# Half of a depthwise convolution moved from GpSimd to TensorE inside a triangular inversion

## The reference, cut to what matters

```python
def _conv_group(z, conv_w, conv_b, ln_g, ln_b):
    u = z[..., :CONV_CH] * jax.nn.sigmoid(z[..., CONV_CH:])
    u = lax.conv_general_dilated(u, conv_w[:, None, :].astype(u.dtype), window_strides=(1,),
                                 padding=[(CONV_K - 1, 0)], dimension_numbers=('NWC', 'WIO', 'NWC'),
                                 feature_group_count=CONV_CH) + conv_b
    return jax.nn.silu(_layernorm(u, ln_g, ln_b))
...
        z = _rms(h, norm1_g[l]) @ w_in[l]
...
        h = h + jnp.concatenate([ya, yr, yc], axis=-1) @ w_out[l]
        h = h + _peer(_rms(h, norm2_g[l]), peer_wq[l], peer_keys[l], peer_u[l], peer_v[l])
```

## Time and profile before

| what | us |
|---|---|
| median of 3 runs | 2104.95 |
| lowest, highest run | 2094.97, 2105.49 |
| profiled execution, its own time | 2105.58 |
| its span | 2103.4 |
| TensorE busy | 1977.3 (94%) |
| VectorE busy | 1459.2 (69%) |
| GpSimd busy | 1279.7 (61%) |
| ScalarE busy | 962.2 (46%) |

### The profile page before, as it was taken

The page is one execution under the profiler, slowest core; times in us unless marked ns, Lnnn a source line. Parts: engine busy times, 40 slices in busy tenths (PEclk is TensorE's granted clock), DMA queues, the critical chain, the costliest instruction groups (busy, mean ns, idle before and its releaser), DMA issues.

```text
span 2103.4 us, 43605 instructions
## 1 busy us (share of the span) xinstructions
PE 1977.3 (94%) x16516; PEld 1889.8 (90%) x16516; DVE 1459.2 (69%) x2757; ACT 962.2 (46%) x1646; POOL 1279.7 (61%) x667
## 2 busy tenths in 40 slices
PE   9957999999999999999999577999999999999999
PEld 8845899999999999999988467999999999999998
DVE  3864419994777788788748535199627777887886
ACT  5422545554333455545554124455543333555553
POOL 5896469998666633233058964799976666332430
PEclk9966899999999999999999678999999999999999
DMA  5300356665444599899743002566555446998995
GB/s 188 102 1 1 92 170 189 181 180 170 151 143 147 180 339 313 288 313 315 249 135 106 1 1 82 179 192 186 183 169 151 145 146 202 349 322 303 323 328 158
DMA packets 106380, 387.80 MB, mean 184 GB/s; under 512 B 11808, under 2 KB 12064, under 8 KB 106016
## 3 DMA queue, kind: packets, MB, share of 16 engines
q1 hardware_dynamic: 87840, 319.25, 47.3%
q0 software_dynamic: 18432, 67.12, 9.2%
HBM read 385.27 MB, written 1.05 MB: 184 GB/s over the span
## 4 chain that ended last, share of the span: by engine, by line
PE 60%; POOL 24%; issue 13%; DVE 2%; ACT 1%; POOLq 0%; ACTq 0%
PE ps L895 60%; POOL w_lo L552 14%; POOL arena L568 6%; POOL arena L577 4%; DVE x L1386 0%; DVE x_lo L1379 0%; POOL arena L564 0%; ACT w_hi L635 0%; DVE onehots_j L1374 0%; DVE h L1816 0%; DVE sel L1702 0%; ACT L759 0%; ACT L610 0%; DVE h L1815 0%; DVE sel L1705 0%
## 5 line engine op out<-in xcount | busy, mean ns | idle before, releaser
L895 PE MATMUL ps<-x_hi,w_hi 128*128 128x240 f32 (+5 forms) x4768 | 1429.3, 324 | 20.4 <-POOL w_lo L552 10.7
L895 PE MATMUL ps<-x_hi,w_lo 128*128 128x240 f32 (+3 forms) x4768 | 1307.3, 274 | 0.0
L552 POOL TENSOR_TENSOR w_lo<-w,w_hi 128x1024 fp32r<-128x1024 f32 x346 | 871.3, 2536 | 390.6 <-ACT w_hi L635 390.0
L895 PEld LDWEIGHTS ps<-x_hi,w_hi 128*128 128x128 f32 x4768 | 904.2, 190 | 73.5 <-POOL w_lo L552 12.6
L895 PEld LDWEIGHTS ps<-x_hi,w_lo 128*128 128x128 f32 x4768 | 909.3, 191 | 0.0
L635 ACT CAST w_hi<-w 128x1024 fp32r<-128x1024 f32 x596 | 623.5, 1046 | 344.3 <-DMA w<-v_c 204.6
L895 PE MATMUL ps<-x_lo,w_hi 128*128 128x240 f32 (+3 forms) x2720 | 757.1, 278 | 0.0
L895 PEld LDWEIGHTS ps<-x_lo,w_hi 128*128 128x128 f32 x2720 | 519.0, 191 | 0.2
L1773 DVE TENSOR_TENSOR w_lo<-w,w_hi 128x1024 fp32r<-128x1024 f32 x250 | 305.6, 1222 | 114.5 <-ACT w_hi L635 113.7
L895 PE MATMUL ps<-arena 64*64 64x64 f32 (+9 forms) x2496 | 176.7, 277 | 60.9 <-ACT arena L783 19.7
L895 PEld LDWEIGHTS ps<-arena 64*64 64x64 f32 (+6 forms) x2496 | 152.0, 172 | 83.7 <-ACT arena L783 20.4
(11 more groups left out here) (187 smaller groups left out, 1691.7 us busy)
## 6 DMA issues: line engine op xcount, KB each, us to landing
w<-u_c SPq DMA_DIRECT2D x256, 512.0 KB, 3.6
w<-v_c SPq DMA_DIRECT2D x256, 512.0 KB, 5.5
w<-w_c SPq DMA_DIRECT2D x84, 512.0 KB, 3.6
arena<-keys_c SPq DMA_DIRECT2D x2, 1024.0 KB, 5.6
arena<-mix_c SPq DMA_DIRECT2D x2, 792.0 KB, 8.2
h<-h SPq DMA_DIRECT2D x2, 544.0 KB, 4.4
out<-x SPq DMA_DIRECT2D x4, 256.0 KB, 2.1
arena<-lora_c SPq DMA_DIRECT2D x2, 256.0 KB, 9.1
```

Source lines behind the costliest of these rows:

```text
L552: g.tensor_tensor(low_of(l, n, wlo_t), low_of(l, n, wraw_t), high_of(l, n).bitcast(F32), ALU.subtract).then_inc(s_lo, 1)
L895: return nc.tensor.matmul(out_, lhsT, rhs, start=start, stop=stop, skip_group_check=True)
```

## The change

The second block of channels (j = 1) is convolved on TensorE. GpSimd builds 31 matrices of 128 by 128, each the identity times one tap's column of weights; they lie in free parts of the arena, of `sel` and of the two one-hot buffers. TensorE multiplies each with the input shifted by the tap and adds all 31 up in bank 6 in fp32. These products stand at fixed places in the inversion (`FILL`): four ahead of level 0, one ahead of each X, two ahead of each pair of updates, until 31 are issued. The update of the second head pair goes to bank 4 in place of 6. ScalarE adds the bias while it copies the result to `cacc`, and TensorE waits for that copy before it uses bank 6 again. The first block stays on GpSimd; its multiplications now have a second operation in each tap (add 0.0), and its additions cover one block. GpSimd splits the low parts of 18 tiles ahead of the convolution, and those of the next three behind it.

```diff
@@ -36,6 +36,10 @@
 LEVELS = (1, 2, 4, 8, 16, 32)
 CONV_K = 31
 CPAD = CONV_K - 1
+TAPS = (12, 6, 7, 6)
+CONV_BANK = 6
+UP_BANKS = (5, 4)
+FILL = (4, 1, 2)
 AH = 8
 
 PH = 8
@@ -283,6 +287,10 @@
 
         ident, ones, iota, fold = res("ident"), res("ones"), res("iota"), res("fold")
 
+        def tap(k):
+            t, i = tap_at[k]
+            return t[:, i * P:(i + 1) * P]
+
         def vcol(l, name, i=0, parts=slice(0, P)):
             a = VEC[name][0] + i
             return vecs[parts, l, a:a + 1]
@@ -327,6 +335,8 @@
         A.at = over_prep
         gram = A.take(NCH * 2 * 4 * CHUNK).rearrange("p (c j m t) -> p c j m t", c=NCH, j=2, m=4)
         cm = A.take(2 * TP).rearrange("p (j c t) -> p j c t", j=2, c=NCH)
+        tap_t = (A.take(TAPS[0] * P), sel_t[:, NR:NR + TAPS[1] * P], ohA_t[:, 0:TAPS[2] * P], ohB_t[:, 0:TAPS[3] * P])
+        tap_at = [(t, i) for t, n in zip(tap_t, TAPS) for i in range(n)]
 
         A.at = over + 6 * T
         vkb = A.take(NCH * 5 * 2 * HD).rearrange("p (c m j n) -> p c m j n", c=NCH, m=5, j=2)
@@ -557,26 +570,20 @@
                 times(pool, n0, n1, lambda n, it: low(l, n, it))
 
             for l in range(DEPTH):
-                lows(l, 0 if l == 0 else AHEAD, NZ + AHEAD)
+                lows(l, 0 if l == 0 else AHEAD, NZ)
 
                 pool.wait_ge(s_ea, l * (NZ + NQ) + ZQ)
                 link(g.memset(cu[:, :, 0:CPAD], 0.0))
                 link(g.tensor_tensor(cu[:, :, CPAD:CPAD + T], z[:, ZCU:ZCU + 2, 1:T + 1], cacc[:, :, :], ALU.mult))
                 for k in range(CONV_K):
-                    for j in range(2):
-                        dst = cacc if k == 0 else ctmp
-                        ins = g.tensor_scalar(dst[:, j, :], cu[:, j, k:k + T], vcol(l, "conv_w", j * CONV_K + k),
-                                              vcol(l, "conv_b", j) if k == 0 else None, ALU.mult,
-                                              *((ALU.add,) if k == 0 else ()))
-                        if j == 0:
-                            ins.then_inc(s_gl, 1)
-                            link.n += 1
-                        else:
-                            link(ins)
+                    g.tensor_scalar(tap(k), ident, vcol(l, "conv_w", CONV_K + k), 0.0, ALU.mult, ALU.add).then_inc(s_tap, 1)
+                for k in range(CONV_K):
+                    link(g.tensor_scalar((ctmp if k else cacc)[:, 0, :], cu[:, 0, k:k + T], vcol(l, "conv_w", k),
+                                         0.0 if k else vcol(l, "conv_b", 0), ALU.mult, ALU.add))
                     if k:
-                        ins = g.tensor_tensor(cacc[:, :, :], cacc[:, :, :], ctmp[:, :, :], ALU.add)
+                        ins = g.tensor_tensor(cacc[:, 0, :], cacc[:, 0, :], ctmp[:, 0, :], ALU.add)
                         link(ins) if k < CONV_K - 1 else ins.then_inc(s_conv, 1)
-                lows(l, NZ + AHEAD, NP)
+                lows(l, NZ, NP)
                 pool.wait_ge(s_ix, l + 1)
                 pool.wait_ge(s_use, l * NW + NV0)
                 pool.wait_ge(s_gm, G0[l + 1])
@@ -783,6 +790,9 @@
                         nc.scalar.copy(xm[:, j], src).then_inc(s_xc, 1)
                     for _ in range(5):
                         after(steps)
+                act.wait_ge(s_cps, l + 1)
+                nc.scalar.activation(cacc[:, 1, :], ps[:, CONV_BANK, 0:T], ACT.Identity,
+                                     bias=vcol(l, "conv_b", 1)).then_inc(s_cpc, 1)
                 for k, (c0, cn, bank) in enumerate(WU):
                     if bank != WU_DVE:
                         act.wait_ge(s_wu, len(WU) * l + k + 1)
@@ -995,6 +1005,15 @@
                     last.then_inc(s_to, 1)
                     yield
 
+            def convolution(l):
+
+                for k in range(CONV_K):
+                    pe.wait_ge(s_tap, CONV_K * l + k + 1)
+                    last = mm(ps[:, CONV_BANK, 0:T], tap(k), cu[:, 1, k:k + T], k == 0, k == CONV_K - 1)
+                    if k == CONV_K - 1:
+                        last.then_inc(s_cps, 1)
+                    yield
+
             def x_split(l, k):
 
                 return lambda c: pe.wait_ge(s_xl, (3 * l + k) * DC + c + 1)
@@ -1104,18 +1123,25 @@
                                  lambda r, j: vtok[r, c, j, :], c % 4 == 0)
                 last.then_inc(s_x0, 1)
                 nlev = len(LEVELS) - 1
+                taps = convolution(l)
+                for _ in range(FILL[0]):
+                    after(taps)
                 for b in range(nlev):
                     for j in range(2):
 
+                        for _ in range(FILL[1]):
+                            after(taps)
                         pe.wait_ge(s_ti, 2 * nlev * l + 2 * b + j + 1)
                         product(3 + j, cm, ti, j).then_inc(s_x, 1)
                     after(steps)
                     for j in range(2):
 
+                        for _ in range(FILL[2]):
+                            after(taps)
                         pe.wait_ge(s_xc, 2 * nlev * l + 2 * b + j + 1)
                         pe.wait_ge(s_tt, 2 * (nlev + 1) * l + 2 * b + j + 1)
                         if b < nlev - 1:
-                            product(5 + j, tt_, xm, j).then_inc(s_up, 1)
+                            product(UP_BANKS[j], tt_, xm, j).then_inc(s_up, 1)
                         after(steps)
                         if b == 0:
                             pe.wait_ge(s_x0c, 2 * (l + 1))
@@ -1136,6 +1162,9 @@
                                 last = mm(ps[r, bank, at:at + P].rearrange("p (m n) -> p m n", m=2), tt_[r, j, c, :],
                                           vkb[r, c, 3:5, j, :], True, True)
                     last.then_inc(s_wu, 1)
+                for _ in taps:
+                    pass
+                pe.wait_ge(s_cpc, l + 1)
                 for c in range(NCH - 1):
                     quads(part(6, c), lambda r, j: vtok[r, c, j, :], lambda r, j: gram[r, c, j, 1, :], c == 0)
                 after(steps)
@@ -1558,7 +1587,7 @@
                             (2 * (2 * nlev - 1) * l + 4 * b + j - 1)
                         if not last:
                             dve.wait_ge(s_up, up + 1)
-                            v.tensor_tensor(ti[:, j], ti[:, j], update(5 + j), ALU.subtract).then_inc(s_ti, 1)
+                            v.tensor_tensor(ti[:, j], ti[:, j], update(UP_BANKS[j]), ALU.subtract).then_inc(s_ti, 1)
                         after(steps)
                         dve.wait_ge(s_up, up + 2)
                         v.tensor_tensor(tt_[:, j], tt_[:, j], update(7 - 7 * j), ALU.subtract).then_inc(s_tt, 1)
```

More of the change, by code:

```diff
@@ L464, in trunk @@
         s_conv = sem("conv_done")
+        s_tap = sem("conv_tap_matrices_ready")
+        s_cps = sem("conv_second_block_in_psum")
+        s_cpc = sem("conv_second_block_copied")
         s_gl = sem("pool_link")
```

## The result

The median of 13 runs is 2112.09 us (2106.14 to 2116.77), against 2103.53 us of 13 runs of the kernel before on the same chips; the ratio is 1.0048 (95% interval 1.0035 to 1.0061). The change made the kernel slower by 0.48%, about 10 us, where 5 us less were forecast. The profiled execution took 2109.26 us, 2107.1 of them span.

What follows compares the result with a forecast made beforehand. VectorE, then TensorE, bounds the inversion; GpSimd's convolution arrives last only once, by 2.00 us. VectorE's relief −11, taps +14.2, clock −8.3 sum to −5.1 us: 2105.58 to 2100.5 us, range 2086 to 2112.

Steps and rivals of the forecast that it cites:

- GpSimd's own times: GpSimd's convolution beside the inversion: rounds about 1.45 us, tap matrices 0.3 to 0.6 us each, end near 135 us.
- The wait for the convolution: TensorE's 2.00 us wait before layer 0's norm sums goes, but not from the path: 0, other end 2 us.
- ScalarE's copy: Copy of the finished block, about 0.4 us, in ScalarE's idle time ahead of the solved pairs: 0, or 0.4 us.
- the three moved subtractions: Three weight subtractions on GpSimd, now behind the convolution, done by 162 us at worst, ahead of the output projection: no cost.
- the net of taps and clock: Inversion on TensorE: taps on the path add 14.2 us, the risen clock gives back 8.3 us.
- VectorE's relief: Inversion: VectorE's instructions meet fewer and shorter GpSimd additions; 2 × (3 + 1.8 + 0.7) = 11 us gained.
- The first stretch: Level 0 and most of level 1, VectorE the path: 3 us gained per layer, ends 0 and 6.2.
- The other parts: VectorE's late delays at L1459 and L1599, 1.8 us per layer, and L1523's form at the start, 0.7.
- The collision model: First 24.5 us: an arriving VectorE instruction loses 0.26 us on average to GpSimd's additions before, 0.16 after.
- the taps lengthen the path: Levels 1 to 3: 16 taps at 0.91 us, no clock regained; +11.8, 2117 us; chance 0.14.

Runs made afterwards that it cites:

- one-tap kernel with late subtractions: The change with one tap product on TensorE in place of 31, and GpSimd's three subtractions held back until ScalarE's copy; 0.9973 of the kernel before, 2096.31 us.
- one tap: The change with one tap product on TensorE in place of 31, subtractions right behind the convolution; 1.0007 of the kernel before, 2102.76 us.
- free places: The change with its 31 taps moved to other places in the inversion; alone 0.9987 of the kernel before, 2096.87 us; with subtractions late 0.9955, 2092.91 us.
- products with zeros: Taps moved, subtractions late, plus 12 zero-matrix products per layer ahead of the updates of levels 1 to 3; 0.9991 of the kernel before, 2097.94 us.
- base: The change with its taps moved to other places in the inversion and the three subtractions late; 0.9955 of the kernel before, 2092.91 us.
- zeros in waits: Taps moved, subtractions late, plus sixteen zero-matrix products per layer where TensorE still waits; 0.9925 of the kernel before, 2087.49 us.
- products alone: The kernel before plus 31 unused tap-sized products, update in bank 4, GpSimd as before; 1.0059 at the change's places, 0.9975 with the taps' moved places.
- slow multiplication: Taps moved, subtractions late, GpSimd's multiplications with one operation again from tap 1 on; 0.9935 of the kernel before, 2089.51 us.

## Why the prediction was wrong, point by point

**GpSimd's own times** came out as predicted: a round of 1.44 us (1.45 forecast), matrices of 0.35 to 0.53 (0.3 to 0.6), the end at 136.0 us (135). L1459's and L1599's forms fell to 0.17 and 0.73 us, as predicted. **The wait for the convolution** (0 to 2 us) and **ScalarE's copy** (0 to 0.4 us) were not measured apart; both are inside the 5.7 us of the one-tap kernel with late subtractions.

**The step that failed first** is the one on the three moved subtractions: "The three subtractions feed the output projection, which comes behind the norm's sums at 192.86 us; they are done by 162 us even at worst". Only their reader was looked at, not the neighbour they would run beside. For 7 us they stand next to VectorE's chain of 8-column instructions and masks, which then take 2.2 to 2.5 us each where 0.17 or 0.5 would do (in layer 1; in layer 0 of the change only one mask, 1.39 us, is seen to suffer). Three pairs of kernels that differ in this alone give 0.28% (change), 0.34% (one tap) and 0.32% (free places): 6 to 7 us where 0 stood.

**The second** is the net of taps and clock, 14.2 − 8.3 = 5.9 us. With both subtractions late, the taps at the change's places cost 1.0020 − 0.9973 = 0.47%, 9.9 us (6.5 to 13 with both intervals). The price of a tap and the worth of the clock can't be told apart in it. The products with zeros give the net by another way: 0.32 us for each of 24, so 10 us for the 32 taps that the forecast had on the path, against 5.9. On the side of the clock, the mean went from 0.70 and 0.71 to 0.82 and 0.81, some 0.4 of the way to full where two thirds were taken, and what a higher clock is worth depends on where it falls: from the base to the zeros in waits it rose from 0.86 to 0.91 in layer 0 and that stage did not get shorter, while the free places alone had 96.02 us at 0.92. The runs do not separate the two. The places were named rightly: 12 + 3 taps free, 16 not. Placing the taps by the waits turned the loss into a gain: 1.0059 to 0.9975 for the products alone; with the real taps the gain over the one-tap kernel, 0.9973 to 0.9955, is within the intervals.

**The third** is VectorE's relief: 11 us predicted, 0.27% or 5.7 us measured. The first stretch, taken at 3 us per layer, gave 24.4 − 23.7 = 0.7. Layer 1 gave 24.5 − 23.7 = 0.8, so 1.5 us came where 6 were forecast. The other parts, 5 us in the forecast, are then worth about 4.2 of the 5.7 us. The collision model had the right mechanism and the wrong size. An addition takes 0.76 us in place of 0.67, and its arrival at random gave VectorE too little delay: of the first ten instructions of level 0 that read SBUF alone, two met an addition for long in the kernel before (1.51 and 1.63 us), and three do in the changed one (0.94, 1.05 and 1.05 us). With the slow multiplication the stretch is 24.4 − 22.3 = 2.1 us shorter, where 3.3 were forecast for that case. That denser additions cost time is what the kernel before with two-operation multiplications shows (0.43%); the 0.20% of the other pair points the same way within the noise.

Sum of the measured terms: −5.7 + 9.9 + 5.9 = 10.1 us, the 0.48% of the ratio. From the −5.1 of the forecast it is 15.2 us away: 5.9 for the subtractions, 4.0 for the taps and the clock, 5.3 for VectorE's relief. (This closes by construction, since the three are differences along one path of kernels; the independent support is in the other pairs, 0.34 and 0.32% for the subtractions and 10 us from the zeros for the taps.) **The rival** that came true in sign is that the taps lengthen the path. It had them at 22.8 us with the clock where it was; they cost 9.9 net with the clock risen, and the subtractions were in no rival. The Trainium skill's rule (TensorE: Matmul & The Clock Gate, "What's actually happening") that activity releases the throttle agrees with the runs: every kernel with 31 products has a mean clock of 0.79 or more in either layer, every one without has 0.73 or less. Its rule on the shared pair of ports (SBUF — State Buffer, "SBUF: two separate sides"), a lock held for the whole instruction, agrees with the additions and subtractions, but not with the multiplications: L1546 took 0.48 us inside a pair of them, and the kernel with twice as long ones was no slower (0.9935 against 0.9955).

## What to carry to other kernels

In this kernel filler products on TensorE paid where it waits longer than they take; ahead of a product that a chain awaits they cost more than the clock they lifted gave back. When a step is moved on GpSimd, look at what VectorE does beside its new place, and hold it back by a wait if that is a chain of small instructions. A faster instruction can be a worse neighbour: what counts is how often an instruction of VectorE starts while GpSimd is in one of those that hold it up, here its additions and subtractions.

## What was not expected of the hardware

Sixteen products with zeros in each layer, in TensorE's waits, shortened the kernel by 0.30%. They compute nothing, so the clock is the only gain that the windows offer (0.80 to 0.87 in layer 1, with 3.5 us), though a kernel with the same products and a fixed clock can't be had to show it. On GpSimd, multiply-and-add takes 0.49 us on 272 columns where multiply alone takes 0.96, and using the faster form made the kernel with both blocks on GpSimd slower by 0.43%; with one block the 0.20% is not clear of noise. A VectorE instruction on 8 columns of 0.17 us takes 2.2 to 2.3 us beside GpSimd's subtraction of 1024 columns. The one-operation form together with the products with zeros was not tried.
